# Conditioning sums of the context: from VectorE to GpSimd in a 13-stage two-block kernel

## What is computed

```python
shift_x, scale_x, gate_x = jnp.split((sc @ ada_w[i] + ada_b[i])[:, None, :], 3, axis=-1)
shift_c, scale_c, gate_c = jnp.split(scc @ ada_w[i] + ada_b[i], 3, axis=-1)
hx = _modulate(x, norm_w[i], shift_x, scale_x)
hc = _modulate(ctx, norm_w[i], shift_c, scale_c)
```

## Time and profile before

| | |
|---|---|
| median of three runs | 2916.75 us |
| profiled execution, span | 2916.6 us |
| TensorE busy | 2776.2 us, 95% |
| VectorE busy | 1820.3 us, 62% |
| ScalarE busy | 1304.8 us, 45% |
| GpSimd busy | 18.4 us, 1% |
| mean granted TensorE clock | 0.976 of full |

### The profile page before, as it was taken

One profiled execution on the slowest core, in us unless ns is written; L12 is line 12 of the kernel. 1 busy time (PEld: TensorE's weight loads), 2 busy tenths in 40 slices (PEclk: granted clock), 3 DMA queues, 4 the chain that ended last, 5 costly groups with the idle time before them and its releaser, 6 DMA issues.

```text
span 2916.6 us, 53037 instructions
## 1 busy us (share of the span) xinstructions
PE 2776.2 (95%) x19577; PEld 2608.2 (89%) x19577; DVE 1820.3 (62%) x2635; ACT 1304.8 (45%) x1674; POOL 18.4 (1%) x33
## 2 busy tenths in 40 slices
PE   5999989999898889999999999999999999999997
PEld 5999779899896789999999998779999999999886
DVE  5776988777777977667763334446454554545544
ACT  4656333454443444334434443444444444444443
POOL 0000000000000000000000000000000000000000
PEclk9999989999898989999999999999999999999999
DMA  5564757676456666766654444664555555555564
GB/s 165 147 195 144 224 181 251 208 227 202 140 178 202 214 192 211 220 190 211 214 182 134 147 140 129 189 186 152 186 181 179 185 178 185 183 182 181 179 185 139
DMA packets 487517, 533.80 MB, mean 183 GB/s; under 512 B 31931, under 2 KB 431814, under 8 KB 486534
## 3 DMA queue, kind: packets, MB, share of 16 engines
q1 hardware_dynamic: 485078, 520.44, 57.2%
q0 software_dynamic: 2064, 10.11, 1.1%
q10 hardware_dynamic: 288, 2.10, 0.2%
HBM read 530.46 MB, written 2.10 MB: 183 GB/s over the span
## 4 chain that ended last, share of the span: by engine, by line
PE 81%; DVE 8%; ACT 3%; DVEq 3%; DMA 2%; issue 2%; SPq 0%; ACTq 0%; POOL 0%; POOLq 0%
PE banks L1692 17%; PE banks L1693 16%; PE banks L1694 16%; PE banks L1700 8%; PE banks L1701 8%; PE banks L1702 8%; DVE w_lo L1112 3%; DMA w_raw<-in_l_w_in 1%; DVE acc_x L1099 1%; ACT w_hi L638 1%; DVEq L1103 1%; PE banks L1846 1%; PE banks L2065 1%; PE banks L2082 1%; DVE acc_c L1099 1%
## 5 line engine op out<-in xcount | busy, mean ns | idle before, releaser
L1112 DVE TENSOR_TENSOR w_lo<-w_raw,w_hi 128x1024 fp32r<-128x1024 f32 (+2 forms) x832 | 967.9, 1178 | 794.8 <-ACT w_hi L638 758.5
L638 ACT ACTIVATE w_hi<-w_raw 128x1024 fp32r<-128x1024 f32 (+2 forms) x832 | 840.9, 1019 | 1069.4 <-PE banks L1694 641.6
L1692 PE MATMUL banks<-act_hl,w_hi 128*128 128x256 f32 x4304 | 1242.6, 289 | 47.0 <-DVE w_lo L1112 22.2
L1694 PE MATMUL banks<-act_hl,w_lo 128*128 128x256 f32 x4304 | 1222.3, 284 | 0.0
L1693 PE MATMUL banks<-act_hl,w_hi 128*128 128x256 f32 x4304 | 1222.1, 284 | 0.0
L1692 PEld LDWEIGHTS banks<-act_hl,w_hi 128*128 128x128 f32 x4304 | 827.8, 192 | 61.6 <-DVE w_lo L1112 21.2
L1693 PEld LDWEIGHTS banks<-act_hl,w_hi 128*128 128x128 f32 x4304 | 828.1, 192 | 3.5 <-issue 2.4
L1694 PEld LDWEIGHTS banks<-act_hl,w_lo 128*128 128x128 f32 x4304 | 828.0, 192 | 0.0
L1700 PE MATMUL banks<-w_hi,act_hl 128*128 128x512 f32 (+3 forms) x1440 | 514.3, 357 | 21.5 <-DVE scr_b L1466 5.9
L1701 PE MATMUL banks<-w_lo,act_hl 128*128 128x512 f32 (+3 forms) x1440 | 510.7, 355 | 0.0
L1702 PE MATMUL banks<-w_hi,act_hl 128*128 128x512 f32 (+3 forms) x1440 | 510.6, 355 | 0.0
(11 more groups left out here) (266 smaller groups left out, 1741.4 us busy)
## 6 DMA issues: line engine op xcount, KB each, us to landing
w_raw<-in_od_w_in SPq DMA_DIRECT2D x256, 512.0 KB, 3.9
w_raw<-in_ev_w_in SPq DMA_DIRECT2D x256, 256.0 KB, 3.6
ada_ring<-in_ada_w SPq DMA_DIRECT2D x192, 256.0 KB, 4.1
w_raw<-in_l_w_in SPq DMA_DIRECT2D x96, 512.0 KB, 5.1
y_mix<-in_ada_w SPq DMA_DIRECT2D x128, 384.0 KB, 4.4
w_raw<-in_l_w_in SPq DMA_DIRECT2D x128, 256.0 KB, 3.4
w_raw<-in_l_w_out SPq DMA_DIRECT2D x64, 512.0 KB, 5.0
w_raw<-in_ev_w_out SPq DMA_DIRECT2D x64, 512.0 KB, 4.6
```

The lines of the kernel that those rows point to most:

```text
L638: nc.scalar.activation(w_hi[:, p % RING, 0:n], w_raw[:, p % RING, 0:n], ACT.Copy)\
L1112: tt(w_lo[:, p % RING, 0:n], w_raw[:, p % RING, 0:n], w_hi[:, p % RING, 0:n].bitcast(F32), ALU.subtract).then_inc(s_lo, 1)
L1692: mm(out, hi, a[:, kt, 0:T], start=start, stop=False, skip_group_check=True)
L1694: return mm(out, lo, a[:, kt, 0:T], start=False, stop=stop, skip_group_check=True)
```

## The change

GpSimd makes the context sums. For each of the 16 groups with a context a new function `context_sums` waits for each of the 8 pieces of `ada_ring`, multiplies its 128x512 (both row tiles, by the two conditioning columns spread over 256) into `acc_c` (piece 0) or a new tile `prod_c`, adds `prod_c` to `acc_c`, and at the end adds the two halves of `acc_c` (128x256) and signals `s_accc`: 8 products, 7 sums of 512 columns, one of 256. Each is followed by a drain but the last. VectorE keeps the sums for `x` and adds the two halves of `acc_x` after the last piece. TensorE's column sums are then one product for each 128 columns of each accumulator, 4 for a group with context in place of 8, and 2 in place of 4 in diff; those of ret stay. A slot of the ring is free once both engines have read it: `s_au` becomes one semaphore for each slot, raised by 1 from either engine, by 2 from VectorE where there is no context.

```diff
--- before.py
+++ after.py
@@ -181,6 +181,7 @@
         ada_ring = sb("ada_ring", [P, ADA_RING, 2 * 256])
         acc_x = sb("acc_x", [P, 2, 256])
         acc_c = sb("acc_c", [P, 2, 256])
+        prod_c = sb("prod_c", [P, 2, 256])
         cn = sb("c_norm", [P, CQ_T + CKV_T, 2 * T], F32R)
         k_raw = sb("k_rope_raw", [64, T])
         k_rot = sb("k_rope", [64, T])
@@ -245,7 +246,8 @@
         s_full = sem("proj_banks_full")
         s_free = sem("proj_banks_free")
         s_aw = [sem(f"ada_landed{k}") for k in range(ADA_RING)]
-        s_au = sem("ada_piece_used")
+        s_au = [sem(f"ada_slot_used{k}") for k in range(ADA_RING)]
+        s_accc = sem("ada_context_summed")
         s_aps = sem("ada_cols_in_psum")
         s_acol = sem("ada_cols_read")
         s_gw = sem("gate_w_landed")
@@ -325,6 +327,8 @@
 
         def ada_buffers(stage):
             return (ada_ring2, acc_x2) if stage == "ret" else (ada_ring, acc_x)
+        CTX0 = {"swa": 0, "out0": 1, "cq": 5, "mla": 8, "out1": 12}
 
         def ada_slab(stage, i, p):
 
@@ -455,8 +459,9 @@
                 u, n = ADA0[stage] + group, ADA_COLS[stage]
                 a = u * 8 + q
 
                 if not isinstance(a, int) or a >= ADA_RING:
-                    sp.wait_ge(s_au, a - (ADA_RING - 1))
+                    sp.wait_ge(s_au[q % ADA_RING], u * 4 + q // ADA_RING * 2)
                 w = d["ada_w_2"].rearrange("l (t p) n -> p l t n", p=P)
                 sp.dma_start(ada_buffers(stage)[0][:, q % ADA_RING, :].rearrange("p (t n) -> p t n", t=2),
                              w[:, 1 if stage == "ret" else 0, 2 * q:2 * q + 2, ds((ADA_FIRST[stage] + group) * n, n)])\
@@ -596,17 +601,47 @@
                 pool.dma_start(gate_w[:, :, 0, :], gx[:, ds(2 * i, 2), :]).then_inc(s_gw, 16)
                 pool.dma_start(gate_w[:, :, 1, :], ga[:, ds(2 * i, 2), :]).then_inc(s_gw, 16)
 
+            def context_sums(stage, group):
+                tt = nc.gpsimd.tensor_tensor
+                for q in range(8):
+                    w = ada_ring[:, q % ADA_RING, :].rearrange("p (t n) -> p t n", t=2)
+                    cond = silu_c[:, 1, 2 * q:2 * q + 2].unsqueeze(2).broadcast_to([P, 2, 256])
+                    pool.wait_ge(s_aw[q % ADA_RING], 16 * ((ADA0[stage] + group) * 2 + q // ADA_RING + 1))
+                    if q == 0:
+                        if stage == "mla" and isinstance(group, int) and group == 0:
+                            pool.wait_ge(s_aps, ADA0["diff"])
+                        elif stage != "swa":
+                            pool.wait_ge(s_aps, ADA0[stage] + group)
+                        tt(acc_c[:, :, :], w, cond, ALU.mult).then_inc(s_au[q % ADA_RING], 1)
+                    else:
+                        tt(prod_c[:, :, :], w, cond, ALU.mult).then_inc(s_au[q % ADA_RING], 1)
+                        nc.gpsimd.drain()
+                        tt(acc_c[:, :, :], acc_c[:, :, :], prod_c[:, :, :], ALU.add)
+                    nc.gpsimd.drain()
+                tt(acc_c[:, 0, :], acc_c[:, 0, :], acc_c[:, 1, :], ALU.add).then_inc(s_accc, 1)
             gates(0)
             with pool.Fori(1, COUNT["lru"]) as i:
 
                 pool.wait_ge(S["lru"]["gates"], i)
                 gates(i)
+            pool.wait_ge(s_pe_, 1)
+            for stage, first, count in (("swa", 0, 1), ("out0", 0, 4), ("cq", 0, 3), ("mla", 0, 1), ("mla", 1, 4), ("out1", 0, 1)):
+                if wanted(stage):
+                    if count - first == 1:
+                        context_sums(stage, first)
+                    else:
+                        with pool.Fori(first, count) as i:
+                            context_sums(stage, i)
             if wanted("ret"):
 
                 pool.wait_ge(s_yl, MIX0["out1"] + len(GROUPS["out1"]))
                 pool.dma_start(ctx_sb, d["ctx_2"].rearrange("o (t p) n -> p (o t) n", p=P)).then_inc(s_ctx, 16)
                 pool.dma_start(gain_bc, d["final_norm_gain"].partition_broadcast(P)).then_inc(s_gain, 16)
 
+                with pool.Fori(1, COUNT["out1"]) as i:
+                    context_sums("out1", i)
                 pool.wait_ge(s_acol, ADA0["ret"])
                 pool.dma_start(const_b[:, :], d["const_b"]).then_inc(s_cb, 16)
@@ -1091,15 +1126,17 @@
                 for t in range(2):
                     kt = 2 * q + t
                     w = ring[:, q % ADA_RING, t * n:(t + 1) * n]
-                    for c, acc in ((1, acc_c), (0, total)) if ada_context(stage) else ((0, total),):
-                        cond, sums = silu_c[:, c, kt:kt + 1], acc[:, t % acc.shape[1], :]
-                        if kt < acc.shape[1]:
-                            last = ts(sums, w, cond, None, ALU.mult)
-                        else:
-                            last = stt(sums, w, cond, sums, ALU.mult, ALU.add)
-                    if t == 0 and acc.shape[1] == 1:
+                    cond, sums = silu_c[:, 0, kt:kt + 1], total[:, t % total.shape[1], :]
+                    if kt < total.shape[1]:
+                        last = ts(sums, w, cond, None, ALU.mult)
+                    else:
+                        last = stt(sums, w, cond, sums, ALU.mult, ALU.add)
+                    if t == 0 and total.shape[1] == 1:
                         drain()
-                last.then_inc(s_au, 1)
+                if q == 7 and total.shape[1] == 2:
+                    drain()
+                    last = tt(total[:, 0, :], total[:, 0, :], total[:, 1, :], ALU.add)
+                last.then_inc(s_au[q % ADA_RING], 1 if ada_context(stage) else 2)
                 drain()
 
             def split(stage):
@@ -1838,13 +1875,13 @@
 
                 stage, group = slab
                 total = ada_buffers(stage)[1]
-                te.wait_ge(s_au, 8 * (ADA0[stage] + group + 1))
+                te.wait_ge(s_au[ADA_RING - 1], 4 * (ADA0[stage] + group + 1))
+                if ada_context(stage):
+                    te.wait_ge(s_accc, CTX0[stage] + group + 1)
                 for b in range(ADA_COLS[stage] // P):
                     for c, acc in enumerate((total, acc_c) if ada_context(stage) else (total,)):
-                        n = acc.shape[1]
-                        for t in range(n):
-                            last = mm(sums[:, 3 * c + b:3 * c + b + 1], acc[:, t, b * P:(b + 1) * P], ones[:, 0:1],
-                                      start=t == 0, stop=t == n - 1, skip_group_check=True)
+                        last = mm(sums[:, 3 * c + b:3 * c + b + 1], acc[:, 0, b * P:(b + 1) * P], ones[:, 0:1],
+                                  start=True, stop=True, skip_group_check=True)
                 last.then_inc(s_aps, 1)
 
             def run(stage):
```

## The result

The changed kernel takes 3017.17 us (median of 4 runs, 3013.66 to 3020.48) against 2916.02 us: the ratio is 1.0349, 95% interval 1.0336 to 1.0363. It is slower by 101 us; forecast was slower by 56. The profiled execution has a span of 3012.9 us, 96.3 more than the 2916.6 of the one before.

A forecast was written before the change was run, and what follows sets the result against it. TensorE, busy 95% of the span, was taken as the bound. Dense groups +58 us, savings in mla and diff -6.8, GpSimd's cost in mla and swa +5: +56 on 2916.6, so 2973 us, range 2888 to 3018.

The forecast's parts named there:

- dense groups: 11 groups in out0, cq and out1, VectorE having 1.6 to 3.3 us to spare: 5.3 us more each, +58 us.
- that step: Whether VectorE and GpSimd run side by side on SBUF: forecast that their two-input times add up, chance 0.53.
- 25.8 and 34.5: Ends for a dense group, in us: VectorE's and GpSimd's times added by streaming alone, or in full; 30 taken.
- The sign "TensorE waiting for GpSimd's acc_c": Expected in the profile after, in out0, cq and out1, with a group period near 30 us.
- GpSimd's price: Each 512-column GpSimd instruction in the context sums takes 1.2 us with its drain, 18.7 us a group.
- The roomy groups: 5 groups, 1 in swa and 4 in mla: 1 us more each for GpSimd's work, +5 us.
- TensorE's 16.8 us: Halved column sums save 13.4 us in 16 groups and 3.4 in diff, all on TensorE's path.
- The chain, the ring and SyncE: GpSimd's sums between TensorE's column sums, slot release and weight loads: 19.7 us against 24.7, so no cost.
- rival 1: VectorE and GpSimd run side by side without stretch in all stages: -24.4 us, 2892 us, chance 0.32.

The follow-up runs named there:

- write-only run: Changed kernel with each of GpSimd's 16 instructions a group replaced by a memset of about the same length, reading nothing: 2896.7 us, and 2888.44 us when run again.
- near-empty kernel: Changed kernel with GpSimd's instructions replaced by memsets of 2 columns (the last keeps 512), same waits and semaphores: 2882.23 us, and 2876.38 us when run again.
- The run behind the rotation: Changed kernel with one more wait: in mla, from the second unit on, GpSimd begins a group only after VectorE's rotation of the queries: 3000.88 us.
- The folding alone: Kernel before, VectorE still making both sums and adding each accumulator's two halves, TensorE making half the column products: 2921.6 us, ratio 1.0019.
- the run without the folding: Changed kernel with context sums on GpSimd, but no sums of halves and 8 column products for a group with context: 3020.37 us, ratio 1.0365.

## Why the prediction was right, and where it was mis-sized

The sign and the mechanism were right, and so was its place for four fifths of the loss: 76.8 of the 96.3 us between the profiled executions came in the 11 dense groups. The size was not: +56 us forecast, +101 measured, at the upper end of the range of 2888 to 3018. Two-input instructions of VectorE and reading instructions of GpSimd exclude each other; the write-only run shows it, and leaves 12 to 14 of the 135 to 141 us between the changed and the near-empty kernel to all other causes. The rule of the Trainium skill that stood beside that step (SBUF — State Buffer, "Who interferes with whom") agrees with the runs, writes included: they spare the two-input forms (1223 ns) and hold up the fast one-input form (715 in place of 346). Its word that the later one blocks agrees too: the GpSimd sum of 2.07 us began when a `w_lo` was under way and ran 0.8 us over its 1.27. It does not by itself give the share of either engine in the turns.

**The dense groups: 5.3 us forecast, 7.0 measured** ((28.5 + 21.0 + 27.3) / 11). I had added up lengths and taken the middle of 25.8 and 34.5, which no row chose; the period is 31.3 to 32.6 us in the two groups of out0 from 334.11 us on. What was missing is the form of turns. VectorE loses 12.1 us in an out0 group: 14 x 0.66 on the sums, 8 x 0.36 on `w_lo`. A short instruction waits as long as a long one. With these measured waits the group closes: VectorE's 23.1 us, less 6.1, plus 0.4, plus 12.1 gives 29.5, and the records show 29.67 of 31.34. The sign "TensorE waiting for GpSimd's acc_c" did not come: what the period waits for is VectorE, and GpSimd's sum is there 7.8 us earlier.

**GpSimd's price: 1.2 us forecast for each instruction, 1.31 measured** from start to start where it is undisturbed. The two memsets of the earlier trace rows and the count of streams gave nearly the right value. Held up by VectorE it is more: in the out0 group the 15 long instructions take 1.47 us each from start to start, and the chain 23.6 us (335.21 to 358.78), over the forecast's 18.7 and its upper end of 21.8.

**The roomy groups: +1 us each for GpSimd in mla and swa forecast; mla took +19.6 in four groups and swa +7.2.** This is the term that failed most: with the column products it stood at +0.6 us for mla and +1 for swa. VectorE had room by the count of busy time, but its two-input rotation stands on TensorE's path. Here is the rotation of one unit of the changed kernel, in order of time; each of the three instructions took 0.67 to 0.68 us before:

```profile
867.07 0.67 DVE L1413 TENSOR_TENSOR scr_a<-banks,const_a 64x512 f32<-64x512 f32 x1
867.67 1.14 DVE L1414 TENSOR_TENSOR scr_a<-scr_a,const_a 64x512 f32<-64x512 f32 x1
868.89 1.37 DVE L1416 TENSOR_TENSOR scr_a<-scr_a 64x512 f32<-64x512 f32 x1
```

The first reads PSUM and keeps its length; the two that read SBUF alone do not. They are 1.15 us longer together; the rest of the 3.1 us of stall comes from the sums and the `w_lo` (1.82 us) in VectorE's queue ahead of them. Over the three units the stalls before the scores grew by 10.1 us and the scores by 10.0, and the two together are about mla's +19.6. The run behind the rotation took both away, but gave back only 7.8 us in mla, since other waits for VectorE took their place. Of swa's 7.2 us, 4.0 are two waits of TensorE for `w_lo` that the kernel before does not have (160 to 292 us); the rest stays open.

**TensorE's 16.8 us: not there.** I put it "all on the path where TensorE is full, and beside no other work". The folding alone gives +6 us instead of -16.8. In out0 its two sums on VectorE lie where VectorE's load counts (+3.0 us of load, +4.0 of time); in mla +8.1 us came at a lower granted clock, for a reason that no run shows. What the folding is worth beside a GpSimd that does not read was not run. In diff, -3.4 was forecast and -4.9 came, though the run without the folding had -3.8 there as well, so little of it is shown to be the folding's.

**The chain, the ring and SyncE: right in the main.** GpSimd idles 7.8 us behind the out0 group shown, and with nothing read the time falls under that of the kernel before. It is not quite free: 12 to 14 us, the stretch of the one-input form included.

Of the rivals, the write-only run is rival 1 brought about: 2888 and 2897 us where I had said 2892. The exclusion decides between the two. That the sum came out so near is in part luck: in the profiled write-only execution out0 and out1 are 17.8 us shorter than before (15.1 forecast), cq 6.6 (2.5), mla 5.0 (3.4) and diff 3.0 (3.4).

## What to carry to other kernels

Work moved to an idle engine is not free if both engines reach memory by the same way: look at what the busy engine's instructions read. Count turns, not lengths: here a short instruction that met a long one waited for the whole of it, so many short ones on the busy side were the worst partners. Ask too whether the busy engine is already what a stage waits for: its share of the whole span (62% here) does not tell. And an engine with room in its busy time can still hold the one instruction that the next engine waits for; there a stall of 3 us was paid twice, once as the stall and once by the clock.

## What the runs showed of the hardware

- A GpSimd instruction on 128x512 fp32 with two inputs takes 1.04 us (a product with a broadcast column) or 1.27 us (a sum of two tiles) undisturbed, with some 0.15 us for the drain between one and the next. A memset takes 1289 ns for 1420 columns, a copy of 1200 columns 1.19 us undisturbed and 1394 ns on average beside VectorE.
- A two-input instruction of VectorE with one input from PSUM keeps its length beside GpSimd's reads (0.67 us at L1413, 867.07 us). Those with two from SBUF wait (1.14 and 1.37 us in place of 0.67 at L1414 and L1416). The fast one-input product of 256 columns (346 ns) waits for writes (715 ns on average in the write-only run) and for reads (523 in the changed kernel).
- In the taking of turns GpSimd is held up far less than VectorE: over the run its instructions average 1211 and 1482 ns, 16 and 17% over their undisturbed length, while VectorE's sums of 479 ns average 834, 74% over.
- In one mla unit, a stretch of 11 us in which TensorE was busy for 8 was followed by 10 us at the granted clock 0.51; the same 16 records of the scores then took 7.54 us and not 4.23.
